# Row capacities in multiples of 16, and a new order at the start and the end of a mixture-of-experts stage

## The chip, the core and the metric

The kernel runs on one core of a Trainium2 chip. The time is that of one execution on the device, in microseconds. TensorE multiplies matrices, VectorE (DVE), ScalarE (ACT) and GpSimd (POOL) work on elements, SyncE (SP) issues loads and stores. Transfers issued by SP and ACT go through hardware queues, those issued by POOL through a software queue; all of them are carried out by the same 16 transfer engines.

## What is computed

One step of a decoder layer for 2048 prompt tokens and 64 sample tokens of width 1024. A token mixer (sliding-window attention beside a short gated convolution) and a layer norm give `h`. Then a mixture of experts and a second layer norm give the result. The part that matters here:

```python
def _routed_experts(xt, eidx, gates, w_gate, w_up, w_down):      # 64 experts, 6 of them per token
    ...
    def step(acc, blk):
        tok, g, e = blk
        xb = xpad[tok]
        hid = jax.nn.silu(xb @ w_gate[e]) * (xb @ w_up[e])       # 1024 -> 256
        yb = (hid @ w_down[e]) * g[:, None]                      # 256 -> 1024
        return acc.at[tok].add(yb.astype(acc.dtype)), None
...
y = _layer_norm(ALPHA * h + moe(h), ln2_g, ln2_b)
```

2112 tokens times 6 are 12672 rows, 198 for an expert on average.

## The kernel before

It has four stages: the mixer (to about 600 us), the dense stage (output projection, first norm, shared expert, router; to about 1015), the experts (to about 2170) and the last norm. Each stage is a block of its own with one instruction list per engine, which ends with all engines meeting at a barrier.

The dense stage writes `h` to `h_d`, the start of the sum (`ALPHA * h` plus the shared expert) to `acc_d`, and for each expert a table of its entries, each a token number and a gate. It orders the experts: the first two are fixed, the others come by rising number of rows. In the expert stage each place in this order has a fixed capacity `n`, from `CLASSES`; rows of an expert beyond its capacity are handled in further blocks behind the 64 experts, in pairs.

An expert's rows are two tiles: tile 0 has 128 rows, tile 1 has `n - 128` (`rows_of`). Experts are handled in pairs (`pair`, with `b` for the one in the pair); TensorE multiplies in three parts, with every operand split in a rounded value and a rest, so weights and rows are rounded by ACT (`round_w`, `round_x`) and the rest is formed by DVE (`split_w`, `split_x`). All of that is in an order written out by hand, with semaphores. For expert `e`:

- SP (L1571, L1576): waits until POOL has kept the entries of expert e-1 (`s_use`), loads the 256 entries into `ent`, then the weights in three loads of 1 MB each as their places come free. These are entries and weights for a place two experts after the one whose buffers they take.
- POOL (L1604 to L1615), one turn for each expert: waits for the entries, gathers the two tiles of rows of `h_d` into `xg` (L1609), then `add_expert` for expert e-3: wait until all earlier additions have landed, copy the row numbers into `rows` (L1587), and for each tile wait for ACT's `y` and add its rows to `acc_d` (L1592, an indirect transfer which adds). Last, `keep_entries` for expert e-1 (L1598) copies `ent` into `use`, and this copy is what SP waits for.
- TensorE: the second half of `gate_up` of expert e-1; for each tile the transposes of the gathered rows into `psX` (L1775) and the tile of `down` of expert e-2 (L1767 to L1769, into `psY`); then the first half of `gate_up` of expert e (L1789, L1791). Tile 1's transposes wait until DVE has read tile 0 out of `psX`.
- ACT: `copy_lo`, `sigmoid`, `hidden`, `round_w`, `round_x`, and `output` (L1670), which scales `psY` by the gate into `y`.

Behind the last pair ACT, DVE, TensorE and POOL finish the last three experts in the order of the lines at the end of each list (`add_expert(e - 3)` to `add_expert(e - 1)`, L1618 to L1622).

The norm stage (`stage_norm`) has 17 tiles of 128 rows. SP loads them from `acc_d`, at most three in flight, and stores the results; ACT loads the two constants `ln2_g`, `ln2_b` and computes the statistics of 15 tiles; DVE computes those of tiles 0 and 8 and all products.

Of the kernel before, what the change touches and what calls it, by code (L numbers as in the profile page):

```python
# [20 lines left out]
I32, U32 = mybir.dt.int32, mybir.dt.uint32  # L21
ACT = mybir.ActivationFunctionType
ALU = mybir.AluOpType
# [31 lines left out]
MORE = NE + 2 * OVMAX  # L55

# [3 lines left out]
CLASSES = ((1, 6, 176), (6, 13, 192), (13, 18, 208), (18, 23, 220), (23, 27, 236), (27, 32, 256))  # L60
# [1436 lines left out]
def stage_experts(nc, io, ov, raw, ent, s_ent, s_w):  # L1497
    PAIRS = NE // 2
    with ExitStack() as ctx:
        ph = Phase(nc, ctx, "ex")  # L1500
        sb, ps, sem = ph.sb, ph.ps, ph.sem
        guh, dnh = sb("guh", [P, 2, KC, 2 * FF], F32R), sb("dnh", [P, 2, FC, D], F32R)
# [20 lines left out]
        rows_of = lambda n, t: P if t == 0 else n - P  # L1523
        exists = lambda e: not (isinstance(e, int) and e < 0)
# [31 lines left out]
        def _(sp):  # L1556
# [21 lines left out]
            pairs(sp, pair)  # L1578

        @block.gpsimd  # L1580
        def _(pool):
            def add_expert(e, b, n):

                if not exists(e):
                    return
                hold(pool, s_add, 32 * e, s_passed)
                nc.gpsimd.tensor_copy(rows[:, 2 * b:2 * b + 2], use[:, 2 * b:2 * b + 2, 0]).then_inc(s_rows, 1)  # L1587
                hold(pool, s_rows, e + 1, s_passed)
                for t in range(2):
                    r = rows_of(n, t)  # L1590
                    hold(pool, s_y, 4 * e + 2 * t + 2, s_passed)
                    nc.gpsimd.indirect_dma_start(  # L1592
                        out=io["acc_d"], out_offset=bass.IndirectOffsetOnAxis(ap=rows[0:r, 2 * b + t:2 * b + t + 1].bitcast(U32), axis=0),
                        in_=y[0:r, 2 * b + t, :], in_offset=None, compute_op=ALU.add).then_inc(s_add, 16)

            def keep_entries(e, b):

                nc.gpsimd.tensor_copy(use[:, 2 * b:2 * b + 2, :], ent[:, 2 * b:2 * b + 2, :]).then_inc(s_use, 1)  # L1598

            def pair(p, n1, n, j):  # L1600
                for b in range(2):
# [16 lines left out]
            add_expert(e - 3, 1, BLK)  # L1618
            keep_entries(e - 1, 1)
            add_expert(e - 2, 0, BLK)  # L1620
            add_expert(e - 1, 1, BLK)
# [3 lines left out]
        def _(act):  # L1625
# [29 lines left out]
            def round_x(e, t, n):  # L1655
# [4 lines left out]
                A(xs[:, :, 0, t * P:t * P + r], psX[:].rearrange("p (k t) -> p k t", k=KC)[:, :, 0:r], ACT.Copy).then_inc(s_xh, 1)  # L1660
# [12 lines left out]
            def pair(p, n1, n, j):  # L1673
                for b in range(2):
# [8 lines left out]
                    round_x(e, 0, n)  # L1683
# [3 lines left out]
                    round_x(e, 1, n)  # L1687
# [18 lines left out]
        def _(dve):  # L1706
# [26 lines left out]
            def split_x(e, t, n):  # L1733
                r = rows_of(n, t)
                dve.wait_ge(s_xh, 2 * e + t + 1)
                V.tensor_tensor(xs[:, :, 1, t * P:t * P + r], psX[:].rearrange("p (k t) -> p k t", k=KC)[:, :, 0:r],  # L1736
                                xs[:, :, 0, t * P:t * P + r].bitcast(F32), ALU.subtract).then_inc(s_xl, 1)

            def pair(p, n1, n, j):
                for b in range(2):  # L1740
# [7 lines left out]
                    split_x(e, 0, n)  # L1748
                    activate(e - 1, 1, m)
                    split_w(e, b, (2,))  # L1750
                    split_x(e, 1, n)
# [11 lines left out]
        def _(pe):  # L1763
# [7 lines left out]
            def transpose_x(p, e, b, t):  # L1771
                pe.wait_ge(s_row[2 * b + t], 16 * (p + 1))
                after(pe, s_xl, 2 * e + t)
                for kc in range(KC):
                    last = nc.tensor.transpose(psX[:, kc * P:(kc + 1) * P], xg[:, 2 * b + t, kc * P:(kc + 1) * P], ident[:])  # L1775
# [222 lines left out]
```

## Time and profile before

| | us |
|---|---|
| median of 3 runs | 2227.34 (2226.11 to 2231.09) |
| profiled execution, its time | 2235.4 |
| its span, from first to last instruction | 2233.9 |
| TensorE busy | 2072.3 (93%) |
| VectorE busy | 1429.2 (64%) |
| ScalarE busy | 1206.0 (54%) |
| GpSimd busy | 590.2 (26%) |
| mean granted TensorE clock | 0.964 of full |

The busy times are of the profiled execution. A share of the span is an average over four stages which have different limits; which engine sets the pace of a stretch is read from the stretch itself. Matmuls are pipelined, so a TensorE which is busy all the time sets the pace without being at its peak. PEclk is the clock that TensorE was granted: 1.00 is 2.4 GHz and 0.50 is 1.2 GHz.

### The profile page before, as it was taken

The page shows a single profiled execution, that of the slowest core. Times are in us where ns is not written, and L with a number is a line of the kernel's source. Part 1 is how long each engine was busy: PE and PEld are TensorE (multiplying, and loading weights), DVE is VectorE, ACT ScalarE, POOL GpSimd, SP SyncE. Part 2 cuts the span into 40 slices and gives each one's busy share as a digit, 9 for nine tenths or more (in the row PEclk, how much of TensorE's full clock was granted, in tenths as well). Part 3 has the DMA queues.
Part 4 walks back from the last instruction along what each step waited for, and adds up shares of the span by engine and source line. Part 5 has one row for each costly group of instructions (what it writes and reads, how often), then busy time and mean ns, then how long its engine had stood idle before and what let it go on. Part 6 is the DMA issues. An engine that isn't in the chain of part 4 may idle for free. (4 is left out here: it accounts for less than half of the span.)

```text
span 2233.9 us, 36439 instructions
## 1 busy us (share of the span) xinstructions
PE 2072.3 (93%) x11572; PEld 1750.4 (78%) x11572; DVE 1429.2 (64%) x2729; ACT 1206.0 (54%) x2122; POOL 590.2 (26%) x662
## 2 busy tenths in 40 slices
PE   6999999999889999985999999999999999999950
PEld 5787787787678888864989899899998878888840
DVE  5444444444567778775677777777777666777728
ACT  4344343343433333323677777777776666766637
POOL 1111111111103232332233333333333334333310
PEclk9999999999899999996999999999999999999985
DMA  6011110100543232345799999999998889999948
GB/s 225 31 42 36 35 36 36 43 29 26 205 151 113 82 106 88 100 151 188 213 311 272 299 281 291 295 277 300 286 274 255 257 264 284 293 284 282 281 73 323
DMA packets 121607, 414.29 MB, mean 185 GB/s; under 512 B 41600, under 2 KB 46208, under 8 KB 95632
## 3 DMA queue, kind: packets, MB, share of 16 engines
q1 hardware_dynamic: 77200, 289.49, 35.1%
q0 software_dynamic: 44048, 122.87, 24.5%
q10 hardware_dynamic: 288, 1.05, 0.1%
q8 instruction: 36, 0.59, 0.1%
q14 instruction: 35, 0.29, 0.0%
HBM read 317.14 MB, written 98.35 MB: 186 GB/s over the span
## 5 line engine op out<-in xcount | busy, mean ns | idle before, releaser
L1789 PE MATMUL ex_psU<-ex_xs,ex_guh 128*128 128x384 f32 (+5 forms) x2048 | 637.7, 374 | 5.5 <-DVE ex_xs L1736 4.7
L1791 PE MATMUL ex_psU<-ex_xs,ex_gul 128*128 128x192 f32 (+5 forms) x2048 | 535.1, 261 | 0.0
L1789 PEld LDWEIGHTS ex_psU<-ex_xs,ex_guh 128*128 128x128 f32 x2048 | 387.0, 189 | 41.4 <-DVE ex_xs L1736 5.4
L1791 PEld LDWEIGHTS ex_psU<-ex_xs,ex_gul 128*128 128x128 f32 x2048 | 392.3, 192 | 2.4
L1592 POOL DMA_INDIRECT acc_d<-ex_y,ex_rows x128 | 209.6, 1638 | 327.8 <-ACT ex_y L1670 299.7
L1609 POOL DMA_INDIRECT ex_xg<-h_d,entries x128 | 143.2, 1119 | 422.8 <-issue 249.9
L1767 PE MATMUL ex_psY<-ex_dnh,ex_hdh 128*128 128x512 f32 (+5 forms) x512 | 212.1, 414 | 0.0
L1769 PE MATMUL ex_psY<-ex_dnh,ex_hdl 128*128 128x512 f32 (+5 forms) x512 | 202.4, 395 | 0.0
L1768 PE MATMUL ex_psY<-ex_dnl,ex_hdh 128*128 128x512 f32 (+5 forms) x512 | 201.6, 394 | 0.0
L1736 DVE TENSOR_TENSOR ex_xs<-ex_psX,ex_xs 128x1024 fp32r<-128x1024 f32 (+5 forms) x128 | 134.3, 1049 | 83.8 <-ACT ex_xs L1660 78.5
L1670 ACT ACTIVATE ex_y<-ex_psY,ex_use 128x512 f32<-128x512 f32 (+5 forms) x256 | 170.5, 681 | 30.2 <-PE ex_psY L1769 29.4
L1713 DVE TENSOR_TENSOR ex_gu<-ex_psU,ex_lo 128x384 f32<-128x384 f32 (+5 forms) x128 | 77.3, 604 | 155.9 <-ACT ex_lo L1632 151.9
L714 PE MATMUL mi_psG<-mi_gh,mi_xh 128*128 128x512 f32 x408 | 167.9, 412 | 2.1 <-DVE mi_gl L536 2.1
L1731 DVE TENSOR_TENSOR ex_gul<-mi_g_raw,ex_guh 128x1024 fp32r<-128x1024 f32 x128 | 156.0, 1219 | 16.4 <-ACT ex_guh L1653 16.2
L1775 PE MATMUL ex_psX<-ex_ident,ex_xg 128*128 128x128 f32 x1024 | 135.2, 276 | 31.9 <-DMA ex_xg<-h_d,entries 26.9
L1731 DVE TENSOR_TENSOR ex_gul<-mi_g_place,ex_guh 128x1024 fp32r<-128x1024 f32 x128 | 156.1, 1219 | 9.0 <-ACT ex_guh L1653 8.4
L714 PE MATMUL mi_psG<-mi_gl,mi_xh 128*128 128x512 f32 x408 | 159.9, 392 | 0.0
L714 PE MATMUL mi_psG<-mi_gh,mi_xl 128*128 128x512 f32 x408 | 159.9, 392 | 0.0
L1632 ACT ACTIVATE ex_lo<-ex_psU 128x384 f32<-128x384 f32 (+5 forms) x128 | 67.0, 524 | 169.5 <-PE ex_psU L1791 166.7
L1775 PEld LDWEIGHTS ex_psX<-ex_ident,ex_xg 128*128 128x128 f32 x1024 | 118.2, 142 | 43.4 <-issue 17.6
L1653 ACT ACTIVATE ex_guh<-mi_g_raw 128x1024 fp32r<-128x1024 f32 x128 | 134.2, 1050 | 17.6 <-PEq L887 17.2
L1660 ACT ACTIVATE ex_xs<-ex_psX 128x1024 fp32r<-128x1024 f32 (+5 forms) x128 | 113.5, 886 | 51.5 <-PE ex_psX L1775 48.8
(366 smaller groups left out, 4176.6 us busy)
## 6 DMA issues: line engine op xcount, KB each, us to landing
mi_g_raw<-w_experts SPq DMA_DIRECT2D x96, 1024.0 KB
mi_g_place<-w_experts SPq DMA_DIRECT2D x96, 1024.0 KB
mi_xr<-xT SPq DMA_DIRECT2D x17, 512.0 KB, 3.6
acc_d<-de_acc SPq DMA_DIRECT2D x17, 512.0 KB, 13.5
h_d<-de_h POOLq DMA_DIRECT2D x17, 512.0 KB
ln_t<-acc_d SPq DMA_DIRECT2D x17, 512.0 KB, 5.9
y<-ln_t SPq DMA_DIRECT2D x17, 512.0 KB, 4.4
de_cr<-cat SPq DMA_DIRECT2D x16, 512.0 KB
```

Source lines behind the costliest of these rows:

```text
L714: last = nc.tensor.matmul(psG[:, (k + j) % 2, :], a[:, k, kc, :], b[:, j, kc, :], start=(kc == 0 and n == 0), stop=(kc == KC - 1 and n == 2))
L1592: nc.gpsimd.indirect_dma_start(out=io["acc_d"], out_offset=bass.IndirectOffsetOnAxis(ap=rows[0:r, 2 * b + t:2 * b + t + 1].bitcast(U32), a ...
L1609: nc.gpsimd.indirect_dma_start(out=xg[0:r, k, :], out_offset=None, in_=io["h_d"], in_offset=bass.IndirectOffsetOnAxis(ap=ent[0:r, k, 0:1]. ...
L1670: A(y[0:r, k, half * 512:(half + 1) * 512], psY[0:r, half, :], ACT.Copy, scale=use[0:r, k, 1:2].bitcast(F32)).then_inc(s_y, 1)
L1731: V.tensor_tensor(lo, src, hi.bitcast(F32), ALU.subtract).then_inc(s_split, 1)
L1736: V.tensor_tensor(xs[:, :, 1, t * P:t * P + r], psX[:].rearrange("p (k t) -> p k t", k=KC)[:, :, 0:r], xs[:, :, 0, t * P:t * P + r].bitcas ...
L1767: nc.tensor.matmul(out, lh, rh, start=start, stop=False)
L1768: nc.tensor.matmul(out, lh, rl, start=False, stop=False)
L1769: return nc.tensor.matmul(out, ll, rh, start=False, stop=stop)
L1775: last = nc.tensor.transpose(psX[:, kc * P:(kc + 1) * P], xg[:, 2 * b + t, kc * P:(kc + 1) * P], ident[:])
L1789: nc.tensor.matmul(psU[:, f, half, 0:2 * n].rearrange("p (s n) -> p s n", s=2), guh[:, b, kc, c0:c0 + P], xs[:, kc, :, 0:n], start=(kc == ...
L1791: last = nc.tensor.matmul(psU[:, f, half, 0:n], gul[:, b, kc, c0:c0 + P], xs[:, kc, 0, 0:n], start=False, stop=(kc == KC - 1))
```

## The change

Five edits:

- **Capacities.** 220 becomes 224 and 236 becomes 240; the last two classes begin one pair later, so that pair 23 has 224 in place of 236 and pair 27 has 240 in place of 256. Tile 1 then has 48, 64, 80, 96, 112 or 128 rows, where before it had 48, 64, 80, 92, 108 or 128.
- **First tiles.** For the first pair of experts tile 1 is transposed into `psY` (which no `down` uses yet) and not into `psX`, and for the second expert of this pair both tiles are transposed before the second half of `gate_up` of the first.
- **Tail order.** Behind the last pair TensorE does tile 0 of expert 62's `down` before the last half of `gate_up` of expert 63, and ACT's `output` of its two units is moved up.
- **Norm's loads.** SP loads norm's constants and its first five tiles at the end of the expert stage, into weight buffers no longer in use; the constants as soon as the last weights are split, the tiles as soon as the last additions have landed (still at most three in flight). The norm stage finds them loaded. ACT does one small `Sqrt` first.
- **Entries between the additions.** POOL copies the row numbers before it waits for the additions of the expert before; and `keep_entries` stands between the two additions of an expert, behind a wait for all four units of `y`.

```diff
-CLASSES = ((1, 6, 176), (6, 13, 192), (13, 18, 208), (18, 23, 220), (23, 27, 236), (27, 32, 256))
+NORM_FIRST, NORM_FLIGHT = 5, 3
+CLASSES = ((1, 6, 176), (6, 13, 192), (13, 18, 208), (18, 24, 224), (24, 28, 240), (28, 32, 256))
...
+        fresh = lambda p: isinstance(p, int) and p == 0
+        rows_T = lambda p, t: psY[:].rearrange("p h n -> p (h n)") if fresh(p) and t == 1 else psX[:]
...
-            pairs(sp, pair)
+            e = 2 * pairs(sp, pair)
+            hold(sp, s_split, 6 * e, s_sp_passed)
+            sp.dma_start(ln_g[:], io["ln2_g"].partition_broadcast(P)).then_inc(s_norm[0], 16)
+            sp.dma_start(ln_b[:], io["ln2_b"].partition_broadcast(P)).then_inc(s_norm[0], 16)
+            hold(sp, s_add, 32 * e, s_sp_passed)
+            for i in range(NORM_FIRST):
+                if i >= NORM_FLIGHT:
+                    sp.wait_ge(s_norm[1 + i % NORM_FLIGHT], 16 * (i // NORM_FLIGHT))
+                sp.dma_start(t_first[:, i], io["acc_d"][i * P:(i + 1) * P]).then_inc(s_norm[1 + i % NORM_FLIGHT], 16)
...
-                hold(pool, s_add, 32 * e, s_passed)
-                nc.gpsimd.tensor_copy(rows[:, 2 * b:2 * b + 2], use[:, 2 * b:2 * b + 2, 0]).then_inc(s_rows, 1)
-                hold(pool, s_rows, e + 1, s_passed)
-                for t in range(2):
-                    r = rows_of(n, t)
-                    hold(pool, s_y, 4 * e + 2 * t + 2, s_passed)
...
+            def add_expert(e, b, n, then):
+                if exists(e):
+                    if not (isinstance(e, int) and e < 2):
+                        hold(pool, s_add, 32 * e - 32, s_passed)
+                    nc.gpsimd.tensor_copy(rows[:, 2 * b:2 * b + 2], use[:, 2 * b:2 * b + 2, 0]).then_inc(s_rows, 1)
+                    hold(pool, s_rows, e + 1, s_passed)
+                    if not (isinstance(e, int) and e < 1):
+                        hold(pool, s_add, 32 * e, s_passed)
+                    add_rows(e, b, 0, n)
+                    hold(pool, s_y, 4 * e + 4, s_passed)
+                then()
+                if exists(e):
+                    add_rows(e, b, 1, n)
...
-                    add_expert(e - 3, 1 - b, n1 if b else n2)
-                    if not (early and e < 1):
-                        keep_entries(e - 1, 1 - b)
+                    add_expert(e - 3, 1 - b, n1 if b else n2, lambda: keep_entries(e - 1, 1 - b))
...
             copy_lo(e - 1, 0, BLK)
             sigmoid(e - 1, 0, BLK)
+            output(e - 2, 0, (0,), BLK)
             hidden(e - 1, 0, 1, BLK)
+            output(e - 2, 0, (1,), BLK)
             copy_lo(e - 1, 1, BLK)
             sigmoid(e - 1, 1, BLK)
-            output(e - 2, 0, range(2), BLK)
             hidden(e - 1, 1, 1, BLK)
...
                 pe.wait_ge(s_row[2 * b + t], 16 * (p + 1))
-                after(pe, s_xl, 2 * e + t)
+                after(pe, s_xl, 2 * e + t - (1 if fresh(p) else 0))
...
-                    gate_up(e - 1, 1 - b, 1, n if b else n1)
+                    if not fresh(p):
+                        gate_up(e - 1, 1 - b, 1, n if b else n1)
                     for t in range(2):
                         transpose_x(p, e, b, t)
                         down(e - 2, b, t, n1)
+                    if fresh(p):
+                        gate_up(e - 1, 1 - b, 1, n)
                     gate_up(e, b, 0, n)
...
             e = 2 * pairs(pe, pair)
+            down(e - 2, 0, 0, BLK)
             gate_up(e - 1, 1, 1, BLK)
-            for t in range(2):
-                down(e - 2, 0, t, BLK)
+            down(e - 2, 0, 1, BLK)
...
-                if i < TILES:
-                    if i >= FLIGHT:
-                        loaded(sp, i - FLIGHT)
-                    sp.dma_start(t[:, i], io["acc_d"][i * P:(i + 1) * P]).then_inc(s_t[i % FLIGHT], 16)
+                if NORM_FIRST <= i < TILES:
+                    loaded(sp, i - FLIGHT)
+                    sp.dma_start(t(i), io["acc_d"][i * P:(i + 1) * P]).then_inc(s_t[i % FLIGHT], 16)
...
-            act.dma_start(lg[:], io["ln2_g"].partition_broadcast(P)).then_inc(s_const, 16)
-            act.dma_start(lb[:], io["ln2_b"].partition_broadcast(P)).then_inc(s_const, 16)
             act.wait_ge(s_var, 1)
+            A(scratch[:, 0, 0:1], eps[:, 0:1], ACT.Sqrt)
+            act.drain()
```

## Rows read from the trace of the kernel before

**Rows 1.** Busy time of the engines (instructions), clock, transfer share, by stretch.

```profile
core 0: us, PE busy (x) PEld busy (x) DVE busy (x) ACT busy (x) POOL busy (x), PEclk, DMA share, GB/s
1400.00:1600.00 200.00, 200.00 (x1249) 180.82 (x1248) 145.28 (x192) 144.47 (x217) 69.47 (x72) 1.00 0.97 290
...
1700.00:1800.00 100.00, 92.18 (x535) 81.40 (x534) 64.66 (x83) 63.75 (x94) 34.46 (x30) 0.97 0.87 259
...
1900.00:2000.00 100.00, 100.00 (x579) 86.96 (x577) 71.82 (x91) 71.02 (x102) 31.75 (x33) 1.00 0.96 299
```

**Rows 2.** TensorE's waits from 1700 to 1900 us: total, times, longest.

```profile
PE ex_psX L1775 <- DMA ex_xg<-h_d,entries: 12.7, 7, 3.6
```

**Rows 3.** Timeline of POOL and SP from 1708: start, duration, instruction, [idle before <-releaser].

```profile
1708.24 1.63 POOL L1592 DMA_INDIRECT acc_d<-ex_y,ex_rows  x1 [1.02 <-issue]
1710.18 1.97 POOL L1592 DMA_INDIRECT acc_d<-ex_y,ex_rows  x1 [0.30 <-issue]
...
1722.76 1.33 POOL L1609 DMA_INDIRECT ex_xg<-h_d,entries  x1 [10.41 <-issue]
...
1857.87 1.83 POOL L1609 DMA_INDIRECT ex_xg<-h_d,entries  x1 [10.62 <-DMA entries<-table]
...
1712.81 0.39 SPq L1571 DMA_DIRECT2D entries<-table  x1
```

**Rows 4.** Timeline of POOL and SP from 1469 to 1497 us.

```profile
1473.87 1.36 POOL L1609 DMA_INDIRECT ex_xg<-h_d,entries  x1 [4.71 <-DMA entries<-table]
...
1479.69 1.61 POOL L1592 DMA_INDIRECT acc_d<-ex_y,ex_rows  x1 [3.02 <-ACT ex_y L1670]
1484.32 1.45 POOL L1592 DMA_INDIRECT acc_d<-ex_y,ex_rows  x1 [3.02 <-ACT ex_y L1670]
...
1496.52 1.61 POOL L1592 DMA_INDIRECT acc_d<-ex_y,ex_rows  x1 [3.02 <-ACT ex_y L1670]
...
1469.62 0.38 SPq L1571 DMA_DIRECT2D entries<-table  x1
```

**Rows 5.** Transfers in 1675:1681, 1653:1658 (queue share), 1665:1870, 1400:1600 (entries, landing).

```profile
q0 software_dynamic: 99, 0.30, 27.2%
...
q0 software_dynamic: 240, 0.85, 90.6%
...
entries<-table SPq DMA_DIRECT2D x11, 2.0 KB, 9.3
...
entries<-table SPq DMA_DIRECT2D x12, 2.0 KB, 3.3
```

**Rows 6.** Timeline of DVE and TensorE in the first pair of experts.

```profile
1028.97 1.22 DVE L1736 TENSOR_TENSOR ex_xs<-ex_psX,ex_xs 128x1024 fp32r<-128x1024 f32 x1 [4.91 <-ACT ex_xs L1660]
...
1034.66 0.80 PE L1789 MATMUL ex_psU<-ex_xs,ex_guh 128*128 128x512 f32 x1 [2.37 <-DVE ex_xs L1736]
...
1052.14 1.07 PE L1775 MATMUL ex_psX<-ex_ident,ex_xg 128*128 128x128 f32 x8 [2.46 <-DVE ex_xs L1736]
...
1055.58 0.79 PE L1789 MATMUL ex_psU<-ex_xs,ex_guh 128*128 128x512 f32 x1 [2.37 <-DVE ex_xs L1736]
```

**Rows 7.** Stretches of the first pair of experts; columns as in rows 1.

```profile
1027.00:1040.00 13.00, 8.17 (x30) 6.62 (x29) 6.99 (x6) 4.88 (x5) 2.73 (x3) 0.50 0.85 294
...
1054.00:1061.00 7.00, 5.42 (x17) 4.64 (x18) 4.96 (x5) 2.47 (x4) 1.06 (x2) 0.51 0.57 191
```

**Rows 8.** Timeline of POOL, SP and ACT from the last additions into the norm stage.

```profile
2151.73 1.57 POOL L1592 DMA_INDIRECT acc_d<-ex_y,ex_rows  x1 [1.19 <-ACT ex_y L1670]
2159.51 0.19 POOL L1587 COPY ex_rows<-ex_use 128x2 int32<-128x2 int32 x1 [6.22 <-DMA acc_d<-ex_y,ex_rows]
2160.66 1.57 POOL L1592 DMA_INDIRECT acc_d<-ex_y,ex_rows  x1 [0.96 <-POOL ex_rows L1587]
...
2173.96 1.29 SPq L1854 DMA_DIRECT2D ln_t<-acc_d  x3
...
2182.12 1.06 ACT L1869 ACTIVATE ln_scratch<-ln_t 128x1024 f32<-128x1024 f32 x1
```

**Rows 9.** Transfer issues of the whole run: count, KB each, median us to landing.

```profile
ln_t<-acc_d SPq DMA_DIRECT2D x17, 512.0 KB, 5.9
```

More of the change, by code:

```diff
@@ L1501, in stage_experts @@
         sb, ps, sem = ph.sb, ph.ps, ph.sem
+        with ExitStack() as overlaid:
+            late = lambda name, shape: overlaid.enter_context(nc.sbuf_tensor(f"ex_{name}", shape, F32))
+            late("front", [P, 12 * D])
+            t_first, ln_g = late("t_first", [P, NORM_FIRST, D]), late("ln_g", [P, D])
+            late("middle", [P, 6 * D])
+            ln_b = late("ln_b", [P, D])
         guh, dnh = sb("guh", [P, 2, KC, 2 * FF], F32R), sb("dnh", [P, 2, FC, D], F32R)
@@ L1596, in keep_entries, with nothing @@
             def keep_entries(e, b):
-                nc.gpsimd.tensor_copy(use[:, 2 * b:2 * b + 2, :], ent[:, 2 * b:2 * b + 2, :]).then_inc(s_use, 1)
+                if exists(e):
+                    nc.gpsimd.tensor_copy(use[:, 2 * b:2 * b + 2, :], ent[:, 2 * b:2 * b + 2, :]).then_inc(s_use, 1)
+            def nothing():
+                pass
             def pair(p, n1, n, j):
@@ L1612, in pair @@
                     n2 = CAPS[2 * p - 4] if early and p > 1 else n1
[L1613 to L1615 removed]
+                    add_expert(e - 3, 1 - b, n1 if b else n2, lambda: keep_entries(e - 1, 1 - b))
             e = 2 * pairs(pool, pair, 2)
[L1618 to L1621, printed above, removed]
+            add_expert(e - 3, 1, BLK, lambda: keep_entries(e - 1, 1))
+            add_expert(e - 2, 0, BLK, nothing)
+            add_expert(e - 1, 1, BLK, nothing)
             hold(pool, s_add, 32 * e, s_passed)
@@ L1653, in round_w, with round_x @@
                     A(hi, src, ACT.Copy).then_inc(s_round, 1)
-            def round_x(e, t, n):
+            def round_x(p, e, t, n):
                 r = rows_of(n, t)
@@ L1659, in round_x @@
                     after(act, s_gu, 2 * e)
-                A(xs[:, :, 0, t * P:t * P + r], psX[:].rearrange("p (k t) -> p k t", k=KC)[:, :, 0:r], ACT.Copy).then_inc(s_xh, 1)
+                A(xs[:, :, 0, t * P:t * P + r], rows_T(p, t).rearrange("p (k t) -> p k t", k=KC)[:, :, 0:r], ACT.Copy).then_inc(s_xh, 1)
             def output(e, b, units, n):
@@ L1682, in pair @@
                     copy_lo(e - 1, 1, m)
-                    round_x(e, 0, n)
+                    round_x(p, e, 0, n)
                     sigmoid(e - 1, 1, m)
@@ L1686, in pair @@
                     output(e - 2, b, (0, 1), n1)
-                    round_x(e, 1, n)
+                    round_x(p, e, 1, n)
                     hidden(e - 1, 1, 1 - b, m)
@@ L1862, in _ @@
             A = nc.scalar.activation
-            act.dma_start(lg[:], io["ln2_g"].partition_broadcast(P)).then_inc(s_const, 16)
-            act.dma_start(lb[:], io["ln2_b"].partition_broadcast(P)).then_inc(s_const, 16)
             act.wait_ge(s_var, 1)
+            A(scratch[:, 0, 0:1], eps[:, 0:1], ACT.Sqrt)
+            act.drain()
             def statistics(i):
                 loaded(act, i)
-                A(scratch[:, 0], t[:, i], ACT.Copy, accum_out=total[:, i:i + 1])
+                A(scratch[:, 0], t(i), ACT.Copy, accum_out=total[:, i:i + 1])
                 act.drain()
@@ L1930, in build @@
         stage_dense(nc, io, ss, ov, front, first_entries, s_ent, s_weights)
-        stage_experts(nc, io, ov, front["raw"], first_entries, s_ent, s_weights)
-        stage_norm(nc, io)
+        s_norm = [sem(n) for n in ("norm_constants", "norm_loaded0", "norm_loaded1", "norm_loaded2")]
+        first = stage_experts(nc, io, ov, front["raw"], first_entries, s_ent, s_weights, s_norm)
+        stage_norm(nc, io, first, s_norm)
 def kernel(x_prompt, x_sample, cache_k, cache_v, state_conv, w_in, attn_sinks, conv_w, g_attn_out, g_conv_out,
```

55 lines of the change are left out of this document (30 added, 25 removed).

## The prediction

> **What bounds the kernel now.** I read first the table of stretches [rows 1]. From 1400 to 1600 us TensorE is busy all the time, so the expert stage runs at TensorE's pace. In 1700 to 1800 us it is not: 92.18 us busy of 100, and PEclk 0.97; from 1900 on it is again. The list of TensorE's waits for 1700 to 1900 us [rows 2] has one entry: transposes (L1775) that waited seven times, 12.7 us in total, for gathered rows.
>
> Who made the rows late? The timeline of POOL and SP [rows 3] shows a closed loop: first addition 1708.24, second addition 1710.18, behind it the copy of `keep_entries`, which lets SP issue the next entries at 1712.81, and only at 1722.76 does POOL gather again, then add again. From there to the gather at 1857.87 it is seven turns, 19.3 us each, of which ten are between the entries' issue and the gather. Some 240 us earlier [rows 4] that wait is 4.25 us, and a turn (first addition to first addition, 1479.69 to 1496.52) 16.8. POOL idles because the load of 2 KB of entries is slow: landing takes 9.3 us (median) in 1665 to 1870 against 3.3 in 1400 to 1600 [rows 5].
>
> Why slow? In 1675 to 1681 us the software queue (gathers and additions) moves 99 packets at 27.2% of 16 engines' time; at 1653 to 1658 the same queue took 90.6% [rows 5]. The second is an addition of expert 35, the last with 208 rows (second tile 80); the first is expert 36's, the first with 220 (second tile 92). 27% of 16 engines is about four. Second tiles of 48, 64 and 80 rows, all multiples of 16, ran before it without this. So I read: a 92-row addition is dealt to four engines, and the entries, which need all 16, end behind it on those four.
>
> **Capacities.** 220 becomes 224 (second tile 96 rows), 236 becomes 240 (112); pair 23 goes from 236 to 224 and pair 27 from 256 to 240. If the lock-in goes, its waits go: 12.7 us [rows 2], and the half-speed clock inside them: PEclk 0.97 over 100 us is 6 us at half speed, 3 us lost [rows 1]. Together -15.7. Price: five pairs gain 4 rows, three gain 4, one loses 12, one loses 16, which is 8 expert-rows in all. If the whole turn grew with the rows that would be 16.8 x 8 / 208 = 0.6 us [rows 4]; part of it doesn't. +0.5.
>
> The Trainium skill has a rule for it, in "DMA: Bandwidth & Descriptors", section "Why a DMA increments its semaphore by 16 and not by 1": a transfer uses the largest number of engines up to 16 that divides its outer dimension, so 92 rows get 4, 108 get 12, 96 and 112 get 16. By it four engines are 25%; the row has 27.2%. It adds one result: tiles of 108 rows hurt little, and the loop should loosen while experts of 236 rows still run; TensorE at 100 of 100 us from 1900 on [rows 1] agrees. Were the cause another, the sum below would lose its first term; by this rule it keeps all of it.
>
> **Copy between the additions.** In the loop of [rows 3] the issue of the second addition, 1.94 us (1708.24 to 1710.18), leaves the way from gather to entries: 19.3 becomes 17.4 a turn, about TensorE's own pace there (16.8 at 208 rows). It is thus a second remedy for the same 15.7 us and adds nothing to the first. In the other stretches the copy waits for y's last unit as the second addition did; entries and three weight loads are issued about one addition's issue (1.45 us, [rows 4]) sooner, with TensorE already 100% busy: nothing. Queued behind the copy is the second addition, later by under 1 us; its landing is next awaited by the following expert's first addition (12.2 us later, 1484.32 to 1496.52) and by ACT's reuse of `y`. Taken at 0.
>
> **First tiles at once.** Today tile 1's transposes wait 2.46 us for DVE to leave psX (as 1052.14 shows for expert 1), and the first matmul 2.37 more [rows 6]. With psY for tile 1, DVE's chain decides: split, weight piece, split, 1.22 each, from 1028.97, so matmuls begin at about 1032.6 instead of 1034.66: -2.1, or half of that if the half-speed clock [rows 7] ends at the same moment as now. For expert 1 the 16 transposes (1.07 us for eight) now stand before `gate_up(0,1)`. ACT's `round_x` stays behind `copy_lo(0,1)`, which needs that block's end. From its end to expert 1's first matmul it is 1.07 + 2.46 + 1.07 + 2.37 = 7.0 us today [rows 6]; without the wait for psX I count 6.2 (DVE: sum, split, activate, weight piece, split). +2.1 - 0.8 = +1.3. Net -0.8 to +0.3, say -0.4. TensorE then idles 6.2 us in one piece, where it now idles twice around a 1.07 us block; should that cost one more stretch at half speed like the 7 us at 1054 to 1061 [rows 7], it adds 3.5. Range -2.5 to +3.5.
>
> **Tail.** TensorE's down of expert 62 tile 0 (twelve matmuls, some 2.7 us) moves ahead of the last `gate_up`, so its addition is issued earlier, but tile 1's units (done just before 2151.73 today, [rows 8]) now stand in ACT's order behind `hidden` of expert 63, which hangs on the delayed `gate_up`: about 1.1 us later. The addition then shares the queue with nothing and lands sooner than today's 7.8 us after issue (2151.73 to 2159.51). I let these cancel, 1.2 either way. The row-number copy leaves the gap between landing and the last additions: 2159.51 to 2160.66, -1.15.
>
> **Norm.** The last addition is issued 1.9 us behind 2160.66 and lands 7.8 later, at about 2170.3. Today: barrier (3.6), SP issues at 2173.96, ACT starts tile 1 at 2182.12 [rows 8], 11.8 us behind the landing; all after it is paced by ACT and DVE and unchanged (51.8 us to the end). New: SP issues at once and the constants are there, but SP may leave the stage only when tile 1 has landed (two waits): 0.4 + 5.9, the median of such a load [rows 9], + 0.4 for one more issue = 6.7. Then the barrier, 3.6 or, with the others long there, less: 2.8. Then 2.0 for tile 0's statistics, the table load beside them. Sum 11.5: -0.3, between -1.4 and +0.6. Most of what the early loads win the later barrier takes back.
>
> **Sum.** -15.7 + 0.5 + 0 - 0.4 - 1.15 - 0.3 = -17.1 us against the profiled execution's own 2235.4 (span 2233.9 and 1.5 around it): 2218.3. That execution lies 8.1 us (0.36%) above the median of 2227.34; in proportion, 2227.34 x 2218.3 / 2235.4 = 2210.3, so 2210 us, 0.8% faster.
>
> **The rivals.**
> (a) The lock-in is shorter without the profiler: part of the 8.1 us is itself this loop. Then at worst 15.7 - 8.1 = 7.6 is there to gain: 2227.3 - 7.6 - 1.4 = 2218. For: timed runs spread from 2226.11 to 2231.09, as a loop with a threshold would. Against: nothing shows that the profiler slows this stage.
> (b) The cause isn't the row count but the load of the transfer engines (busy 0.97 at 208 rows, [rows 1]), and the loop comes back at 224 rows with entries just as much later as they are issued sooner. Only head and tail are left: 2225 to 2227. Against: at 0.96 in 1900 to 2000, with larger tiles, TensorE is 100% busy.
> (c) Slower: the second addition now starts beside the weights' 3 MB and not ahead of them. POOL holds the next expert's first addition until it has landed. Today 12.2 us lie between them, and up to three more are hidden, since the second then waits for y anyway (3.02 us, [rows 4]); if landing takes over 15 us, every expert pays the excess. 1 us over is 61 us, less 17: 2271. Against: landing is 7.8 us today with another addition ahead of it [rows 8]; even doubled packets' time stays under 15.
> (d) A lower capacity that an expert exceeds: one more pair of blocks, at least two turns of 17 us: 2244. The reference's routing of these inputs puts 214 rows at most in pair 23 (new 224) and 231 in pair 27 (240). All but excluded.
>
> **How the numbers follow.** Forecast 0.77 (its own range 2205 to 2214), (a) 0.13, (b) 0.05, (c) 0.02, (d) under 0.01, the rest unforeseen, to either side. The range goes from 2203 (head -2.1, tail and norm -2.3 beyond the sum, 3 for what a free loop may give elsewhere) to 2219 (rival (a), or the forecast with head +3.9, tail +1.2 and norm +0.9 beyond the sum and some of (a)). 0.2% is 4.5 us, about what a measurement of this kernel can tell from no change: faster 0.92, same 0.05, slower 0.03.
>
> **What would show it.** Entries land in 3 to 5 us at every expert; no wait of the transposes for gathered rows behind the first pair; TensorE busy 100 of 100 us in 1600 to 2100; DMA share above 0.9 there. Head: the first matmul 2 us earlier, one gap of about 6 us before expert 1's. Tail: last additions back to back, norm's first load issued before the barrier, ACT's tile 1 about 1 to 2 us earlier against the last landing. Wrong would be: entries at 9 us behind 96-row additions, additions that land over 15 us after issue, or a longer half-speed stretch at the head.

## The result, and the profile after

The changed kernel takes 2201.35 us (median of four runs, 2201.2 to 2204.78) beside 2227.17 for the kernel before on the same chip: ratio 0.9885, 95% interval 0.9867 to 0.9902, so 25.8 us or 1.15% faster. The forecast was 2210 with a range from 2203 to 2219: the sign is right, and the time lies 1.7 us below the range. Below, a landing is the end of a transfer, counted from its issue where a length is given.

First the stretches of after, to be held against [rows 1, 7]:

```profile
core 0: us, PE busy (x) PEld busy (x) DVE busy (x) ACT busy (x) POOL busy (x), PEclk, DMA share, GB/s
1027.00:1040.00 13.00, 10.63 (x52) 9.35 (x52) 6.73 (x7) 5.00 (x7) 3.35 (x3) 0.69 0.87 297
1054.00:1061.00 7.00, 7.00 (x38) 6.10 (x37) 1.93 (x3) 1.99 (x4) 0.00 (x0) 0.89 0.75 288
1700.00:1800.00 100.00, 100.00 (x605) 89.72 (x604) 72.15 (x93) 71.64 (x104) 42.70 (x36) 1.00 0.95 289
```

In 1700 to 1800 us TensorE is busy for all 100 us at full clock, where before it was busy for 92.18 at 0.97. The list of TensorE's waits from 1050 to 2150 us says the same: the wait for gathered rows of [rows 2] is gone, and what is left is one wait in the first pair and one of 1.2 us in the tail.

```profile
PE ex_psU L1818 <- DVE ex_xs L1765: 6.0, 1, 6.0
PE ex_psY L1796 <- ACT ex_y L1698: 1.2, 1, 1.2
PE ex_psY L1796 <- issue: 0.7, 1, 0.7
```

One turn of POOL and SP in the same place, from the timeline (compare [rows 3]), and the landing of the entries in 1665 to 1870 us (9.3 us before, [rows 5]):

```profile
1713.46 1.61 POOL L1603 DMA_INDIRECT acc_d<-ex_y,ex_rows  x1 [5.53 <-ACT ex_y L1698]
1717.36 0.56 POOL L1626 COPY ex_use<-entries 128x4 int32<-128x4 int32 x1 [2.29 <-ACT ex_y L1698]
1718.18 1.49 POOL L1603 DMA_INDIRECT acc_d<-ex_y,ex_rows  x1 [0.26 <-issue]
1721.16 1.01 POOL L1640 DMA_INDIRECT ex_xg<-h_d,entries  x1 [1.50 <-issue]
...
1718.29 0.38 SPq L1580 DMA_DIRECT2D entries<-table  x1
```

```profile
entries<-table SPq DMA_DIRECT2D x12, 2.0 KB, 1.9
```

The gather follows the entries' issue by 2.9 us (before: ten), and POOL's long wait is now for ACT's `y`, so TensorE sets the turn: 1713.46 to 1730.76, 17.3 us.

The first pair, to be held against [rows 6]:

```profile
1025.10 1.97 PE L1804 MATMUL ex_psY<-ex_ident,ex_xg 128*128 128x128 f32 x8 [0.65 <-DMA ex_xg<-h_d,entries]
...
1028.16 1.23 DVE L1765 TENSOR_TENSOR ex_xs<-ex_psY,ex_xs 128x1024 fp32r<-128x1024 f32 x1 [0.25 <-ACT ex_xs L1688]
1029.44 0.79 PE L1818 MATMUL ex_psU<-ex_xs,ex_guh 128*128 128x512 f32 x1 [2.37 <-DVE ex_xs L1765]
...
1051.14 0.80 PE L1818 MATMUL ex_psU<-ex_xs,ex_guh 128*128 128x512 f32 x1 [5.96 <-DVE ex_xs L1765]
```

And the end, against [rows 8]: the last additions, SP's five early loads, ACT's table load and its first statistics (tile 1).

```profile
2128.41 1.55 POOL L1603 DMA_INDIRECT acc_d<-ex_y,ex_rows  x1 [5.91 <-ACT ex_y L1698]
...
2135.47 1.55 POOL L1603 DMA_INDIRECT acc_d<-ex_y,ex_rows  x1 [5.31 <-DMA acc_d<-ex_y,ex_rows]
2137.33 1.55 POOL L1603 DMA_INDIRECT acc_d<-ex_y,ex_rows  x1 [0.30 <-issue]
...
2144.40 4.84 SPq L1595 DMA_DIRECT2D ex_t_first<-acc_d  x5
...
2149.66 1.28 ACT L1901 ACT_TABLE_LOAD   x1 [16.14 <-PEq L1500]
...
2151.52 1.04 ACT L1906 ACTIVATE ln_scratch<-ex_t_first 128x1024 f32<-128x1024 f32 x1
```

From the issue of the last addition to SP's first load it is 7.07 us (before 11.42, 2162.54 being the last addition), and to ACT's first statistics 14.19 (before 19.58). So 5.4 us were won behind the last addition, where the forecast had 0.3.

To find where the rest came from, I took from each trace the start of every expert's first transpose. The table gives the distance of these between places in the order of experts (counted from 0), in us; "turn" is the distance of two neighbours.

| | before | after | difference |
|---|---|---|---|
| place 0 to 2 (first pair) | 43.31 | 41.88 | -1.4 |
| 2 to 36 | 556.89 | 557.07 | +0.2 |
| 36 to 50 | 260.20 | 243.27 | -16.9 |
| 50 to 62 | 220.11 | 217.61 | -2.5 |
| turn at 220 rows before the loop, and at 224 | 17.15 | 17.33 | +0.18 |
| turns that end at places 42 to 49 | 18.76 to 20.98 | 17.30 to 17.74 | |
| turn at 236, and at 240 | 17.85 | 17.77 | -0.08 |

The two profiled spans differ by 30.8 us (2233.9 and 2203.1) and the medians by 25.8. Of the 5 us between, 3.4 lie ahead of the expert stage, in code that the change leaves alone: place 0 begins at 1025.91 before and at 1022.48 after, and at 1018 to 1025.4 in the kernels below. Another 1.4 are an addition that landed later than usual in the profile of before (8.93 us between the first addition of expert 63 and the one ahead of it; 7.2 to 7.6 in the other kernels with that order).

### The profile page after: what moved, and what is told of

The parts are those of the page before. It is cut to its first block and busy times, and to the rows that moved or that the text cites. A ratio compares the mean times of both kernels' runs of the same rounds, so it can differ in the third digit from the quotient of the medians.

```text
span 2203.1 us, 36568 instructions
## 1 busy us (share of the span) xinstructions
PE 2063.7 (94%) x11572; PEld 1748.2 (79%) x11572; DVE 1431.6 (65%) x2729; ACT 1206.0 (55%) x2123; POOL 649.0 (29%) x662
## 5 line engine op out<-in xcount | busy, mean ns | idle before, releaser
L1603 POOL DMA_INDIRECT acc_d<-ex_y,ex_rows x128 | 199.5, 1558 | 394.6 <-ACT ex_y L1698 348.3
L1640 POOL DMA_INDIRECT ex_xg<-h_d,entries x128 | 151.6, 1184 | 154.2 <-issue 99.3
L1698 ACT ACTIVATE ex_y<-ex_psY,ex_use 128x512 f32<-128x512 f32 (+5 forms) x256 | 170.8, 680 | 27.7 <-PE ex_psY L1798 27.3
L1765 DVE TENSOR_TENSOR ex_xs<-ex_psX,ex_xs 128x1024 fp32r<-128x1024 f32 x126 | 131.9, 1047 | 64.4 <-ACT ex_xs L1688 63.0
L1681 ACT ACTIVATE ex_guh<-mi_g_raw 128x1024 fp32r<-128x1024 f32 x128 | 134.2, 1050 | 15.3 <-PEq L888 15.3
L1681 ACT ACTIVATE ex_guh<-mi_g_place 128x1024 fp32r<-128x1024 f32 x128 | 134.4, 1050 | 0.0
```

Of the source, the lines that this page charges most:

```text
L1603: nc.gpsimd.indirect_dma_start(out=io["acc_d"], out_offset=bass.IndirectOffsetOnAxis(ap=rows[0:r, 2 * b + t:2 * b + t + 1].bitcast(U32), a ...
L1640: nc.gpsimd.indirect_dma_start(out=xg[0:r, k, :], out_offset=None, in_=io["h_d"], in_offset=bass.IndirectOffsetOnAxis(ap=ent[0:r, k, 0:1]. ...
L1681: A(hi, src, ACT.Copy).then_inc(s_round, 1)
L1698: A(y[0:r, k, half * 512:(half + 1) * 512], psY[0:r, half, :], ACT.Copy, scale=use[0:r, k, 1:2].bitcast(F32)).then_inc(s_y, 1)
```

## The experiments

Each kernel is the one before or the one after with the edit shown; ratios are to the kernel before on the same chip, with a 95% interval in brackets, and gains in us are worked out from the ratio.

**Capacities alone.** The kernel before with this line:

```diff
-CLASSES = ((1, 6, 176), (6, 13, 192), (13, 18, 208), (18, 23, 220), (23, 27, 236), (27, 32, 256))
+CLASSES = ((1, 6, 176), (6, 13, 192), (13, 18, 208), (18, 24, 224), (24, 28, 240), (28, 32, 256))
```

> The kernel before with the new capacities alone. Theory: the closed loop of entries, gather and additions in experts 36 to 53 came from tiles of 92 and 108 rows, and cost more than the waits listed: in the two traces the distance between the transposes of expert 36 and those of expert 50 shrinks by 16.9 us, and by 18.7 if the four more rows per expert are counted. With pairs 23 and 27 at a lower capacity about 1.5 us more: -18.5 us, 2208 to 2210. Rival: the loop was freed by the copy between the two additions, or by both together; then the capacities alone give less than 10 us, and entries behind additions of 96 rows land in more than 7 us.

Measured: 2209.74 us, ratio 0.9903 (0.9888 to 0.9918), -21.6 us. TensorE's list has no wait for gathered rows, the entries land in 3.7 us, and place 36 to 50 takes 243.17 us. From place 2 to 62 it saves 19.1 us on the profile of before. The capacities alone free the loop.

**The copy alone.** POOL's part of the diff in the kernel before, with capacities 220 and 236.

```diff
+                    add_rows(e, b, 0, n)
+                    hold(pool, s_y, 4 * e + 4, s_passed)
+                then()
+                if exists(e):
+                    add_rows(e, b, 1, n)
```

> The kernel before with only the copy of row numbers moved ahead and the entries kept between an expert's two additions. As predicted: it is a second remedy for the same loop, 19.3 us a turn becomes 17.4, so nearly all of the loop's cost goes with capacities unchanged: -13 to -18 us, 2209 to 2214, though entries still land late (9 us). Rival: the issue of the entries comes sooner but they then land beside the second addition's trickle, so the turn stays near 19 us: 0 to -3 us.

Measured: 2262.7 us, ratio 1.013 (1.0114 to 1.0147): 29 us slower. Neither expectation had this sign. TensorE's waits from 1700 to 1900 us, and a turn of POOL and SP there:

```profile
PE ex_psX L1789 <- DMA ex_xg<-h_d,entries: 32.5, 9, 5.2
```

```profile
1759.60 0.76 POOL L1612 COPY ex_use<-entries 128x4 int32<-128x4 int32 x1
1760.57 1.98 POOL L1589 DMA_INDIRECT acc_d<-ex_y,ex_rows  x1 [0.21 <-issue]
1765.93 1.02 POOL L1626 DMA_INDIRECT ex_xg<-h_d,entries  x1 [3.39 <-issue]
1767.26 1.19 POOL L1626 DMA_INDIRECT ex_xg<-h_d,entries  x1 [0.30 <-issue]
1768.46 1.19 POOL L1599 COPY ex_rows<-ex_use 128x2 int32<-128x2 int32 x1
1781.01 1.63 POOL L1589 DMA_INDIRECT acc_d<-ex_y,ex_rows  x1 [11.35 <-issue]
...
1760.83 0.39 SPq L1574 DMA_DIRECT2D entries<-table  x1
1761.55 1.66 SPq L1579 DMA_DIRECT2D mi_g_raw<-w_experts  x3
```

The entries now come soon enough: issued at 1760.83, gathered from at 1765.93. But the second addition, 92 rows issued at 1760.57, is followed within 1 us by 3 MB of weights, and POOL can issue the next expert's first addition only at 1781.01, 20.4 us later, with 11.35 us of idle time before it. That a landing ends this wait the list of POOL's waits shows (four of them, 46.3 us, named as waiting for the addition's landing, the others with no releaser). The turn shown is 22.5 us, and place 36 to 50 takes 290.93 us, 30.7 more than in before. This is rival (c) of the prediction, on the old capacities.

**The copy left out of the change.** The kernel after with POOL's list of before.

```diff
-                    add_expert(e - 3, 1 - b, n1 if b else n2, lambda: keep_entries(e - 1, 1 - b))
+                    add_expert(e - 3, 1 - b, n1 if b else n2)
+                    if not (early and e < 1):
+                        keep_entries(e - 1, 1 - b)
```

> The kernel after with the entries kept behind both additions again, as before. With 92-row tiles this part alone cost 1.3% (33.7 us of waits). Theory: the cost was the second addition's 20 us of landing on four engines beside the weights' loads; at 96 to 128 rows on 16 engines it lands in under 12 us and nothing waits for it, so leaving this part out changes nothing: 2199 to 2204, same periods for each expert within 0.05 us. Rival: it costs something in every expert, or helps the new capacities run free of waits: more than 5 us either way, or waits of the transposes for gathered rows appear.

Measured: 2201.48 us (0.9876, 0.9859 to 0.9892) beside 2201.35 for the whole change; from place 36 to 50 it takes 243.13 us (after: 243.27), with no wait of TensorE but the one in the tail. In the change the copy between the additions costs and gives nothing.

**Which row counts are bad.** The kernel before with second tiles of 104 and then 116 rows.

```diff
+CLASSES = ((1, 6, 176), (6, 13, 192), (13, 18, 208), (18, 24, 232), (24, 28, 244), (28, 32, 256))
```

> The kernel before with capacities 232 for pairs 18 to 23 and 244 for pairs 24 to 27, so second tiles of 104 and then 116 rows. Theory, the largest divisor up to 16: 104 rows go to 13 engines, 116 to 4. So experts 36 to 47 run without the loop, at 17.5 us each, entries landing in under 5 us, and the loop appears at experts 48 to 55: waits of the transposes for gathered rows there of 5 us or more. Rival, only multiples of 16 are good: the loop already stands in experts 36 to 47, with over 10 us of waits there. Rival, it is the count of rows or bytes that matters: no loop in either.

Measured: 2232.04 us (1.0014, 1.0004 to 1.0025), and the loop is where the number of engines says it should be. Landing of the entries from 1650 to 1850 us (104 rows), then from 1850 to 2020 (116 rows), and TensorE's waits in the second stretch; in the first that list is empty.

```profile
entries<-table SPq DMA_DIRECT2D x11, 2.0 KB, 4.4
...
entries<-table SPq DMA_DIRECT2D x8, 2.0 KB, 10.6
```

```profile
PE ex_psX L1778 <- DMA ex_xg<-h_d,entries: 8.5, 4, 3.3
```

At 232 rows a turn is 17.55 to 17.75 us; at 244 it is 17.9 at first and then 20.7 to 21.4. Neither a multiple of 16 is needed (104 is none) nor are many rows the trouble. The Trainium skill, "DMA: Bandwidth & Descriptors", section "Why a DMA increments its semaphore by 16 and not by 1", has it that the largest divisor up to 16 of the outer dimension sets the number of engines: 13 for 104, 4 for 116 as for 92. By that rule the loop belongs at 116 and not at 104, and the trace agrees.

The share of the software queue in stretches in which a second tile is under way shows the number itself. In turn: 104 rows (this kernel, 1721 to 1723 us), 108 rows (before, 1952 to 1955) and 116 rows (this kernel, 1971 to 1974).

```profile
q0 software_dynamic: 62, 0.25, 78.7%
...
q0 software_dynamic: 123, 0.34, 78.8%
...
q0 software_dynamic: 56, 0.14, 26.5%
```

Thirteen engines of 16 would be 81%, twelve 75% and four 25%. The tiles of 108 rows also rule out a reading that I had not put to the test, that a tile has to be a multiple of 8 rows: 108 is none, yet in the kernel before the turn is 17.85 us with them, the entries land in 4.7 us (1905 to 1985), and TensorE is busy for 60 of 60 us from 1925 to 1985.

**Only the gathers made up.** The kernel before; gathers fetch 96 and 112 rows, additions keep 92 and 108.

```diff
-                        k, r = 2 * b + t, rows_of(n, t)
+                        k, r = 2 * b + t, -(-rows_of(n, t) // 16) * 16
```

> The kernel before with only the gathers of 92 and 108 rows made up to 96 and 112 (four more rows are fetched and not used); additions keep 92 and 108. Theory: the entries wait behind the second addition's tile of 92 rows, issued just before them, so the loop stays: 0 to -4 us, entries land in 8 to 10 us. Rival: the gathers' tiles are what comes late; then 10 us or more are gained.

Measured: 2226.78 us (0.9987, 0.9978 to 0.9997), -2.9 us with 0.7 to 4.9 as bounds; entries still at 9.4 us, TensorE's waits 11.6 us in seven times. So the gathers' tiles do not make the loop. That leaves the additions, whose tile stands ahead of the entries; additions made up to 96 rows beside gathers of 92 were not run.

**Norm's loads alone.** The norm part of the diff (constants and five tiles loaded at the end of the expert stage, ACT's early `Sqrt`) in the kernel before.

```diff
+            hold(sp, s_add, 32 * e, s_sp_passed)
+            for i in range(NORM_FIRST):
...
+                sp.dma_start(t_first[:, i], io["acc_d"][i * P:(i + 1) * P]).then_inc(s_norm[1 + i % NORM_FLIGHT], 16)
```

> The kernel before with only norm's loads at the end of the expert stage. The trace of after shows ScalarE's first statistics 14.2 us after the last addition where before it was 19.6; if that is the early loads' doing, this gives -5.4 us: about 2221.8. Rival, the prediction's term: -0.3 us (-1.4 to +0.6), the rest of the gain at the end being the tail order's.

Measured: 2225.6 us (0.9973, 0.9963 to 0.9984), -6.0 us. From the last addition's issue to ACT's first statistics it is 14.16 us, as in after (14.19), so the whole gain at the end of after is here. Why, the list of what the barrier's line executes shows, an engine's own bookkeeping that is not counted as busy time (columns: count, shortest, median and longest in ns, start in us). In the kernel before, then in the one after:

```profile
L1499 POOLq DRAIN  x1: 4181/4181/4181, 2169.5 to 2169.5; - x1
```

```profile
L1500 POOLq DRAIN  x1: 3654/3654/3654, 2144.4 to 2144.4; - x1
L1500 SPq DRAIN  x1: 123/123/123, 2149.3 to 2149.3; - x1
```

What I had read as a barrier of 3.6 us is POOL's drain: it begins at 2169.5, 0.4 us behind the last packet of the last addition (2169.1), takes 4.18 us, and only then (2173.96) could SP load. In after SP begins at 2144.40, beside POOL's drain, and the barrier behind SP's last load takes 0.4 us (2149.24 to 2149.66). Three kernels test this.

**The drain moved ahead of the wait**, in the kernel before:

```diff
             add_expert(e - 1, 1, BLK)
+            pool.drain()
             hold(pool, s_add, 32 * e, s_passed)
```

> The kernel before with one drain of POOL put ahead of its last wait for the additions. In the trace of before POOL's drain at the end of the stage takes 4.18 us behind the landing, and norm's first load is issued 4.85 us behind it. Theory: this drain is work of POOL's that could as well be done while the last addition is under way; then norm's first load comes under 1 us behind the landing and ScalarE's first statistics at 9 instead of 13.0. Rival: a drain behind a wait for additions costs its 4 us whatever came before: the load stays at 4.2 to 4.9 us.

Measured, one run: 2226.44 us. The drain at the barrier and SP's first load:

```profile
L1499 POOLq DRAIN  x1: 53/53/53, 2164.6 to 2164.6; - x1
```

```profile
2164.91 9.99 SPq L1855 DMA_DIRECT2D ln_t<-acc_d  x6
```

The drain at the barrier is now 0.05 us. The load comes 3.2 us behind the last packet of the last addition, not 4.85: between the two expectations, as the early drain itself ends only 2.7 us behind that packet. So it is 1.7 us of gain and not 4.

**Three tiles ahead of the barrier**, on the kernel after, first without and then with the line of the drain:

```diff
-            for i in range(NORM_FIRST):
+            for i in range(3):
...
+            pool.drain()
             hold(pool, s_add, 32 * e, s_passed)
```

> The kernel after with three instead of five of norm's tiles loaded ahead of the barrier, so that SP waits for no landing. Theory: POOL's drain (3.65 us) then decides the barrier: VectorE's first statistics at 4.3 to 5 us behind the last landing, where after has 5.76, ScalarE's at 6 to 6.9 instead of 7.56. Rival: the barrier costs 0.8 us behind SP whatever POOL does: VectorE begins when tile 0 has landed, at 3.7, ScalarE at 5.4.

> The same with POOL's drain ahead of its last wait as well. Theory: nothing is left of the barrier but 0.8 us behind SP's third load (2.1 us behind the last landing), so VectorE begins when tile 0 has landed, 3.7 us behind it, and ScalarE at 5.4. Rival: as without it, 4.3 to 5 and 6 to 6.9.

Measured, one run each: 2201.19 and 2202.87 us, which says nothing at this size; the rows do. Without the drain moved:

```profile
2142.13 1.28 SPq L1595 DMA_DIRECT2D ex_t_first<-acc_d  x3
...
2146.12 1.29 DVE L1929 BATCH_NORM_STATS2 ln_st<-ex_t_first 128x6 f32<-128x512 f32 x2
...
2147.92 1.04 ACT L1906 ACTIVATE ln_scratch<-ex_t_first 128x1024 f32<-128x1024 f32 x1
```

```profile
L1500 POOLq DRAIN  x1: 3654/3654/3654, 2142.1 to 2142.1; - x1
```

And with it:

```profile
2144.63 1.28 SPq L1595 DMA_DIRECT2D ex_t_first<-acc_d  x3
...
2147.81 1.29 DVE L1930 BATCH_NORM_STATS2 ln_st<-ex_t_first 128x6 f32<-128x512 f32 x2 [1.38 <-DMA ex_t_first<-acc_d]
...
2149.61 1.04 ACT L1907 ACTIVATE ln_scratch<-ex_t_first 128x1024 f32<-128x1024 f32 x1
```

SP's first load marks the landing. From it to ACT's first statistics: 7.12 us in after, 5.79 with three tiles, 4.98 with the drain moved as well. In the first of the two VectorE starts 0.3 us behind the end of POOL's drain (2142.1 + 3.65); in the second it waits 1.38 us for tile 0 itself, so tile 0's own load is what is left between the landing and VectorE. Counted from the last packet of the last addition, 0.4 us ahead of SP's load, VectorE starts at 4.4 and 3.6 us and ACT's statistics at 6.2 and 5.4: the first theory's expectations hold in both.

**The first pair alone.** `rows_T`, `fresh` and the order of `gate_up` in the kernel before.

```diff
+                    if fresh(p):
+                        gate_up(e - 1, 1 - b, 1, n)
                     gate_up(e, b, 0, n)
```

> The kernel before with only the first pair's change (second tile transposed into the other bank, and both tiles ahead of the last half of expert 0). Prediction: -0.4 us (-2.5 to +3.5). From the first transposes to those of expert 2 the kernels without this edit took 41.6 to 43.6 us in their profiles, the one after 41.9; so the rival is that the edit is worth nothing at all and what the two traces differ by there is the clock's own variation: this stretch within 41.6 to 43.6, time within 2 us of before.

Measured: 2227.8 us (0.9995, 0.9986 to 1.0004): the time can't tell. The traces can, taken together. Place 0 to place 2 takes, with the old order, 43.31, 43.64, 43.41 and 42.95 us or 41.89, 41.64, 42.02 and 41.91; with the new one 41.88 and 41.77 or 40.29, 40.27 and 40.49. Each order has two levels about 1.5 us apart, and one kernel with the new order, the last one below, came in between with 40.82. Two things differ in these stretches. TensorE stands idle for 9.7 us from place 0 to place 2 in each of the eight kernels with the old order, and for 8.7 to 9.0 us in the six with the new one: 0.7 to 1.0 us is the edit's. The rest goes with the granted clock: with the old order it is 0.75 or 0.76 in the four slower kernels and 0.77 or 0.78 in the others, with the new one 0.77 in the two slower and 0.82 in the others. At 0.77 the two orders take about the same time (41.9 to 42.0 against 41.8 to 41.9). In four of the six with the new order the clock is near full for some 4 us from about 4 us behind place 0 (0.92 from 1024 to 1028 in this kernel) and falls again; in the other two, and in all eight with the old order, it is 0.50 there. That points at a part of the order in the clock, but no run tests it. The rival, that the edit is worth nothing, is out: 40.29 lies below its 41.6, and the idle time is shorter each time.

**The tail order alone.**

```diff
+            down(e - 2, 0, 0, BLK)
             gate_up(e - 1, 1, 1, BLK)
-            for t in range(2):
-                down(e - 2, 0, t, BLK)
+            down(e - 2, 0, 1, BLK)
```

> The kernel before with only the order of the last steps on TensorE and ScalarE changed (the row-number copy stays where it was). Prediction: the delay of expert 62's second tile and the faster landing of its first cancel: 0, between -1.2 and +1.2. Rival: the gain at the end is this order's, since fewer additions stand behind each other at the last: -3 us or more.

Measured: 2233.05 us (1.0005, 0.9995 to 1.0014). From the transposes of expert 63, expert 62's second addition is issued at 27.7 to 27.9 us in the five kernels with the new order and at 26.5 to 27.0 in the nine with the old one, which is about 1 us later; the first of expert 63 follows 7.7 us behind it here and about 7.5 with the old order. So nothing is won back by a faster landing. The row-number copy ahead of the wait gives about 0.3 us at most: between these two additions it is 7.1 to 7.4 us in four kernels that have it and 7.6 in a fifth (the last one below), and 7.5 to 7.7 in eight that don't (the 8.93 of before aside).

**What the runs point to.** The kernel after with more fitting capacities, three tiles, the drain moved and the old tail order:

```diff
+CLASSES = ((1, 6, 176), (6, 13, 192), (13, 21, 208), (21, 24, 224), (24, 29, 240), (29, 32, 256))
```

> The kernel after, with four changes that the runs point to: capacities 208 up to pair 20, 224 for pairs 21 to 23, 240 up to pair 28 and 256 for the last three (places 36 to 41 have 208 rows at most in this input, places 56 and 57 up to 236); three of norm's tiles ahead of the barrier; POOL's drain ahead of its last wait; and the tail order of before. By the rows: six experts at 16.88 instead of 17.33 is -2.7, two at 17.77 instead of 18.5 is -1.5, the two at norm -2.1, the tail order -0.9: -7.2 us, 2194 (2191 to 2199). Rival: the loop returns, or a wait, where an expert's work gets shorter; then 2200 or more.

Measured: 2193.18 us (2191.77 to 2196.56), ratio 0.9844 (0.9831 to 0.9858), 8 us below the changed kernel, or 9 by the two ratios, since the chips differ. The turn that ends at place 42 is 16.90 us and that at place 58 is 17.77, and from SP's first load to ACT's first statistics it is 5.0 us.

## Why the prediction was right in its cause and wrong in its size

The terms as the prediction put them, and as the rows and runs have them:

| term | predicted | measured | from |
|---|---|---|---|
| loop of entries and additions | -15.7 | -17.4 | place 36 to 50, 260.2 us, less ten turns of 17.14 and four of 17.85 |
| rows of the new capacities | +0.5 | -1.8 | +0.2, +0.5 and -2.5 in the three stretches; 0.4 of it is spread between traces |
| copy between the additions | 0 | 0 | change without it, 2201.48 |
| first pair | -0.4 | -1.4 | 43.31 to 41.88 us; 0.7 of it TensorE's idle time |
| row copy ahead of the wait | -1.15 | -0.3 | 7.1 to 7.4 us (once 7.6) against 7.5 to 7.7 |
| tail order | 0 | +1.0 | second addition of expert 62 |
| norm | -0.3 | -5.4 | 19.58 to 14.19 us |
| sum | -17.1 | -25.3 | medians: -25.8 |

**Norm: the step that failed.** The prediction wrote "barrier (3.6), SP issues at 2173.96" and, for the new order, "Then the barrier, 3.6 or, with the others long there, less: 2.8", and closed that the later barrier takes back most of the early loads' gain. There was no such barrier. The time is POOL's drain of 4.18 us, which starts at the landing and not at the end of SP's loads, so it now runs beside them and costs nothing: from the end of SP's loads to VectorE's start it is 0.5 us where the forecast had 2.8. That is 2.3 us of the 5.1 that were missed. Of the rest, 1.2 are on the side of before, where ACT's first statistics came 13.0 us behind the landing and not 11.8 (the last addition landed at about 2169.1 and not 2170.3), 1.4 are SP's part (from the landing to the end of its five loads 5.3 us and not 6.7), and 0.2 the step from VectorE's start to ACT's statistics (1.8 us and not 2.0). The drain's rows show the first point in every trace: 2.75 to 4.19 us in the eleven kernels without an earlier drain, 0.05 in the three with one. The others are read from the two traces.

**Capacities: the cause right, two sizes too small.** Four engines for 92 rows, the entries stuck behind them, the closed loop and its end: all of it as predicted, and the test with 104 and 116 rows separates it from its rivals. The loop was costlier than its waits: 12.7 us of waits and 3 of half clock make 15.7, while the turns lost 17.4 in the profile of before and 17.5 to 19.8 in the four other kernels with these capacities and POOL's order (260.3 to 262.6 us from place 36 to 50). The difference of 1.7 us lies in TensorE's busy time. From 1626.11 to 1886.31 us, place 36 to 50 of before, it is 247.5 us; fourteen turns without the loop are 242.8, so 4.7 more, of which the half clock accounts for 3. What makes the rest stays open. The other size is that of the rows. "+0.5" took every row of an expert as 0.08 us. In the turns a row is worth 0.045: +0.18 for four rows at ten experts (+1.8), 17.85 to 17.3 for twelve at pair 23 (-1.1 for its two experts), 18.53 to 17.77 for sixteen at pair 27 (-1.5). That alone, for the eight rows in all, would have left the term at +0.4. But the six experts that go from 236 to 240 cost nothing, they take 0.08 us less each (-0.5 where this price gives +1.1). The list of matmuls says where: in `gate_up` those with 236 columns take 273 ns on average and those with 240 take 269, while 472 and 480 columns take 383 both, and an expert has 32 of each. Why fewer columns are not faster there the runs don't say. Places 56 to 62 take 111.0 us instead of 111.6 with their rows unchanged, but that is not the change's: in five of the six other kernels with the old capacities they take 111.1 to 111.3. Nor is the +0.2 from place 2 to 36, where all fourteen kernels lie between 556.7 and 557.1.

**The rivals.** Rival (a), a loop that is shorter without the profiler, is refuted: the capacities alone give 21.6 us in the medians (18.3 to 25.0) and 19.1 in the profile. The sum's last step, in proportion to an execution 8.1 us above the median, was harmless; of these 8.1 us about 5 are the late start and the slow addition named above. Rival (b), that the load of the transfer engines makes the loop and 224 rows bring it back, is refuted by the entries' landing of 1.9 us. For (d), an expert beyond its capacity, there is no further pair of blocks in the trace.

**Copy between the additions: right in the sum, wrong in its reason.** "A second remedy for the same 15.7 us" is refuted: alone it costs 29 us. It takes the issue of the second addition out of the way of the entries as counted, and puts the addition on four engines beside 3 MB of weights, with the next expert's first addition behind it. Rival (c) had this mechanism and its point of decision right (a landing of over 15 us; it was about 20), and at 0.02 its chance was fair for 16 engines only.

**First pair: -1.4, inside the range given.** The matmul came 6.96 us behind the first transposes (1022.48 to 1029.44) where before it was 8.75 (1025.91 to 1034.66), less 1.8; expert 1's single idle time of 5.96 us is the 6.2 counted. A longer half-speed stretch did not come: in four of the six kernels with the new order there is one more (PEclk 0.54 from 1028 to 1031 in the first pair alone), but it follows an early full-speed one, and the mean clock from place 0 to place 2 is higher there, 0.82.

**Tail.** -1.15 was too much and 0 too little: together they came to +0.7, since the later second tile ("about 1.1 us later", measured 1.0) is real and the faster landing that was to cancel it isn't.

**The range** failed at its low end because it held 2.3 us for tail and norm beyond the sum, and norm alone went 5.1 beyond it.

## What to carry to other kernels

Give every transfer that others queue behind an outer dimension with a large divisor: four rows more cost 0.2 us in an expert here, and the four engines cost 17 to 20 us from place 36 to 50, and 48 once their transfer stood beside 3 MB of other loads. A reordering which is harmless or useful on 16 engines can be the dearest of all on four, so parts of a change that seem to be remedies for the same fault are each to be tried alone. Before a gap in front of a stage is called a barrier, look at what each engine executes on the barrier's line: here the work that only POOL does there was hidden by letting SP's loads go first.

## What the runs showed that was not expected

- POOL's drain behind indirect additions takes 2.75 to 4.19 us when it follows their landing (eleven kernels), and 0.05 when another stood ahead of the wait (three kernels); the early one ends 2.7 us behind the last packet in the kernel before and about 1 us in the two built on the one after. What sets its length is not shown.
- Experts with 240 rows take 17.77 us a turn and with 236 17.85, in every trace; with 244, before the loop set in, 17.9.
- The start of the expert stage, behind unchanged code, varies from 1018 to 1026 us between kernels, and the first pair has two levels 1.5 us apart at the same order; an effect of 1 us is readable from a stretch in several traces and not from a total.
